# Value columns of an input projection as three split products: the order of work around them and a weight split moved to the next stage

## What is computed

```python
z, xbc, dt_raw, q, k, v, g_out, gk_low = jnp.split(h @ p['w_in'], offsets, axis=-1)
xbc = jax.nn.silu(conv_fn(xbc, p['conv_w'], p['conv_b']))
...
gf = jax.nn.log_sigmoid((gk_low @ p['gk_up_f'] + p['gk_bias_f']).astype(f32)) / GLA_GATE_NORM
...
'v': heads(v, GLA_HEADS, GLA_VAL_DIM),
```

## Time and profile before

| what | value |
|---|---|
| median of 3 runs | 2380.34 us (2379.8 to 2381.73) |
| profiled execution | 2379.42 us, its span 2377.7 us |
| mean granted TensorE clock | 0.949 of 2.4 GHz |
| TensorE (PE) busy | 2166.9 us, 91% |
| VectorE (DVE) busy | 1637.9 us, 69% |
| ScalarE (ACT) busy | 1137.4 us, 48% |
| GpSimd (POOL) busy | 512.4 us, 22% |
| projection, first feature product to first chunk work | 54.1 to 604.1 us of the span |

### The profile page before, as it was taken

How to read it: one execution, slowest core, us unless ns; L and a number is a source line. 1 busy time by engine, 2 the same in 40 slices (tenths; PEclk the granted TensorE clock), 3 DMA queues, 4 the chain that set the end, 5 groups by cost and what they waited for, 6 DMA issues and landing times. The chain is left out here.

```text
span 2377.7 us, 36401 instructions
## 1 busy us (share of the span) xinstructions
PE 2166.9 (91%) x11761; PEld 1711.5 (72%) x11761; DVE 1637.9 (69%) x2101; ACT 1137.4 (48%) x1477; POOL 512.4 (22%) x535
## 2 busy tenths in 40 slices
PE   4999999999899997999997389999999999999980
PEld 2776777777677776888886277787877878878760
DVE  1333333333677667777772889999999999999983
ACT  0222222222555552333332067777777777777763
POOL 1000000000001003233231023333332334334332
PEclk7999999999999996999998699999999999999995
DMA  8223334331598869998873637469978779899957
GB/s 323 67 67 118 117 113 140 119 127 56 182 332 304 293 211 316 315 309 288 301 254 73 233 88 235 129 215 291 327 237 273 222 242 374 273 318 316 373 170 296
DMA packets 208013, 537.25 MB, mean 226 GB/s; under 512 B 14768, under 2 KB 45483, under 8 KB 201387
## 3 DMA queue, kind: packets, MB, share of 16 engines
q1 hardware_dynamic: 174904, 424.71, 49.9%
q0 software_dynamic: 30512, 102.77, 16.5%
q10 hardware_dynamic: 2499, 8.45, 0.9%
HBM read 402.28 MB, written 133.61 MB: 225 GB/s over the span
## 5 line engine op out<-in xcount | busy, mean ns | idle before, releaser
L2180 ACT ACTIVATE w_hi_e<-w_gates 128x2048 fp32r (+1 forms) x103 | 197.9, 1923 | 212.3 <-issue 103.4
L2306 DVE TENSOR_TENSOR w_lo_e<-w_gates,w_hi_e 128x2048 fp32r<-128x2048 f32 x103 | 236.4, 2296 | 33.9 <-ACT w_hi_e L2180 33.9
L2306 DVE TENSOR_TENSOR w_lo_e<-w_ups,w_hi_e 128x2048 fp32r<-128x2048 f32 x102 | 233.3, 2288 | 35.8 <-ACT w_hi_e L2180 35.8
L2306 DVE TENSOR_TENSOR w_lo_e<-w_downs,w_hi_e 128x2048 fp32r<-128x2048 f32 x100 | 228.4, 2284 | 0.0
L2180 ACT ACTIVATE w_hi_e<-w_ups 128x2048 fp32r (+1 forms) x102 | 195.7, 1919 | 23.7 <-PE pd_e L2253 22.5
L2180 ACT ACTIVATE w_hi_e<-w_downs 128x2048 fp32r x100 | 191.6, 1916 | 0.7
L614 PE MATMUL pf<-raws,w_in_sb 128*128 128x256 f32 x800 | 179.0, 387 | 1.1 <-DVE raws L695 1.1
L2253 PE MATMUL pg_e<-w_hi_e,x_hi_e 128*128 128x512 f32 x408 | 167.1, 409 | 7.4 <-DVE w_lo_e L2306 7.4
L614 PEld LDWEIGHTS pf<-raws,w_in_sb 128*128 128x128 f32 x800 | 155.2, 195 | 23.4 <-DVE raws L695 1.5
L2158 POOL DMA_INDIRECT x_mid<-yb_e,to_e x50 | 127.5, 2551 | 187.2 <-DVE yb_e L2350 185.0
L2253 PE MATMUL pd_e<-w_hi_e,h_hi_e 128*128 128x512 f32 x400 | 162.2, 406 | 0.0
(11 more groups left out here) (429 smaller groups left out, 4711.1 us busy)
## 6 DMA issues: line engine op xcount, KB each, us to landing
w_gates<-in_w_gate_dram SPq DMA_DIRECT2D x32, 2048.0 KB, 12.0
w_ups<-in_w_up_dram SPq DMA_DIRECT2D x32, 2048.0 KB
w_downs<-in_w_down_dram SPq DMA_DIRECT2D x32, 2048.0 KB
w_mod_half<-in_w_mod_dram SPq DMA_DIRECT2D x16, 1024.0 KB, 6.6
abc_m<-a_rows SPq DMA_DIRECT2D x16, 1024.0 KB, 4.8
recs<-tok_rec SPq DMA_DIRECT2D x15, 968.0 KB, 7.8
qk_rec<-qk SPq DMA_DIRECT2D x14, 1024.0 KB, 3.9
qk<-qk_rec SPq DMA_DIRECT2D x14, 1024.0 KB
```

The costliest lines, as they stand in the source:

```text
L2180: act.activation(w_hi[:, s % 3:s % 3 + 1, :], raw(part, half, place), ACT.Copy).then_inc(hi_done, 1)
L2306: dve.tensor_tensor(w_lo[:, s % 3:s % 3 + 1, :], raw(part, half, place), w_hi[:, s % 3:s % 3 + 1, :].bitcast(F32), ALU.subtract).then_inc( ...
```

## The change

It does four things.

- The values become split products. `w_in_sb` ends ahead of the value columns. The value weight comes in four chunks of two row blocks through `w_raw`, at the start of `projection`, and is split into `wv_hi` and `wv_lo` (ScalarE, VectorE) in the context group. Each half of a group's tokens is split into `x_hi` and `x_lo` (one buffer each), and the three products go into the same `pz`.
- The first half's values move on TensorE from behind `psm` to between the feature pairs 3 and 4; the transposes of the next inputs stand ahead of the second half's values.
- On ScalarE the second half's high part, SiLU and the next inputs' squares stand ahead of the eviction of feature pair 4.
- `KA` is 0: all 8 row blocks of the gate weight are split in `chunks`; blocks 0 to 2 are loaded in the last but one group of `projection`.

```diff
-KA = 3
+KA = 0
...
-W_LEN = O_G - O_XBC
+W_LEN = O_V - O_XBC
...
-                sp.dma_start(w_in_sb[:, k, :], A["w_in"][0][k * P:(k + 1) * P, O_XBC:O_G]).then_inc(w_in_loaded, 16)
+                sp.dma_start(w_in_sb[:, k, :], A["w_in"][0][k * P:(k + 1) * P, O_XBC:O_V]).then_inc(w_in_loaded, 16)
...
+            def load_v(c):
+                if c >= 3:
+                    sp.wait_ge(wv_lo_done, c - 2)
+                for n in range(2):
+                    k = 2 * c + n
+                    sp.dma_start(w_raw[c % 3][:, n, :], A["w_in"][0][k * P:(k + 1) * P, O_V:O_G]).then_inc(wv_loaded[c % 3], 16)
+            for c in range(3):
+                load_v(c)
...
             sp.dma_start(slab[:, :, :], w_mod_d[EARLY][0]).then_inc(slab_loaded, 16)
+            load_v(3)
...
-                if it == SPLIT - 1:
+                if it == LAT_GROUPS - 1:
+                    sp.wait_ge(wv_lo_done, PAIRS)
                     for k in range(3):
                         load_w(k)
-                if SPLIT <= it < LAT_GROUPS:
-                    sp.wait_ge(K["w_lo_done"], it - SPLIT + 1)
-                    load_w(it - SPLIT + 3)
...
+            def high(it, buf, s):
+                if s:
+                    act.wait_ge(tok_ps, it * 2 + 1)
+                else:
+                    act.wait_ge(ht_done, it * 4 + 4)
+                    if not it == 0:
+                        act.wait_ge(tok_ps, it * 2)
+                act.activation(x_hi[:, :, :], hT[buf][:, :, s * P:(s + 1) * P], ACT.Copy).then_inc(x_hi_done, 1)
+
             def body(it, use, buf, is_ctx, after):
 
+                high(it, buf, 0)
+                if is_ctx:
+                    for c in range(PAIRS):
+                        act.wait_ge(wv_loaded[c % 3], 32 * (c // 3 + 1))
+                        act.activation(wv_hi[:, 2 * c:2 * c + 2, :], w_raw[c % 3], ACT.Copy).then_inc(wv_hi_done, 1)
                 for n in range(5):
+                    if n == 4:
+                        high(it, buf, 1)
+                        act.wait_ge(conv_done, it + 1)
+                        act.activation(fm[:, 0:6, :], fm[:, 0:6, :], ACT.Silu).then_inc(silu_done, 1)
+                        if after is not None:
+                            head(*after)
                     act.wait_ge(feat_ps, it * 5 + (n + 1))
...
-                act.wait_ge(conv_done, it + 1)
-                act.activation(fm[:, 0:6, :], fm[:, 0:6, :], ACT.Silu).then_inc(silu_done, 1)
-                if after is not None:
-                    head(*after)
...
+            def values(it, s, is_ctx):
+                if s == 0 and not is_ctx:
+                    pe.wait_ge(min_done, it * 4)
+                    pe.wait_ge(abs_done, it * 4)
+                if is_ctx:
+                    pe.wait_ge(wv_lo_done, PAIRS)
+                pe.wait_ge(x_lo_done, it * 2 + s + 1)
+                for k in range(KT):
+                    for j, (a, b) in enumerate(((x_hi, wv_hi), (x_hi, wv_lo), (x_lo, wv_hi))):
+                        mm = pe.matmul(pz[s][:, :], a[:, k, :], b[:, k, :], start=(k == 0 and j == 0), stop=(k == KT - 1 and j == 2))
+                mm.then_inc(tok_ps, 1)
...
                 for n in range(5):
+                    if n == 4:
+                        values(it, 0, is_ctx)
...
-                for s in range(2):
...
-                    for k in range(KT):
-                        mm = pe.matmul(pz[s][:, :], h[:, k, s * P:(s + 1) * P], w[:, k, O_V - O_XBC:O_V - O_XBC + GW],
-                                       start=(k == 0), stop=(k == KT - 1))
-                    mm.then_inc(tok_ps, 1)
-                    if after is not None:
-                        turned(*after, range(2 * s, 2 * s + 2))
+                if after is not None:
+                    turned(*after, range(0, 2))
+                values(it, 1, is_ctx)
+                if after is not None:
+                    turned(*after, range(2, 4))
...
+            def low(it, buf, s):
+                dve.wait_ge(x_hi_done, it * 2 + s + 1)
+                dve.tensor_tensor(x_lo[:, :, :], hT[buf][:, :, s * P:(s + 1) * P], x_hi[:, :, :].bitcast(F32), ALU.subtract).then_inc(x_lo_done, 1)
...
+                low(it, buf, 0)
+                if is_ctx:
+                    for c in range(PAIRS):
+                        dve.wait_ge(wv_hi_done, c + 1)
+                        dve.tensor_tensor(wv_lo[:, 2 * c:2 * c + 2, :], w_raw[c % 3], wv_hi[:, 2 * c:2 * c + 2, :].bitcast(F32),
+                                          ALU.subtract).then_inc(wv_lo_done, 1)
...
+                low(it, buf, 1)
                 dve.wait_ge(small_ps, it + 1)
...
-            for k in range(KA + NW, KT):
+            for k in range(NW, KT):
                 sp.wait_ge(w_lo_done, k - NW + 1)
                 load_w(k)
...
-            weights(range(KA, KA + NW))
+            weights(range(NW))
...
-                    weights(range(KA + NW, KT))
+                    weights(range(NW, KT))
```

More of the change, by code:

```diff
@@ L143, in placed @@
             return [where.enter_context(nc.sbuf_tensor(f"{name}{b}", shape, dt, side=side)) for b in range(n)]
-        F32R = mybir.dt.float32r
         recs = placed(spans, "right", "recs", 1, [P, 3 * T_LEN])[0]
@@ L149, in build @@
              "hT": raws[:, 3 * D:].rearrange("p (k c) -> p k c", k=KT),
-             "w_hi": placed(early, "left", "w_zg_hi", 1, [P, KA, 2, SW], F32R),
-             "w_lo": placed(early, "left", "w_zg_lo", 1, [P, KA, 2, SW], F32R),
              "nega": placed(early, "left", "nega", 1, [P, 2 * SH])[0]}
@@ L410, in projection @@
         a_loaded, a_exp, a_done = (sem(n) for n in ("a_loaded", "a_exp", "a_done"))
-        w_raw, w_hi, w_lo = K["w_raw"], K["w_hi"][0], K["w_lo"][0]
-        SPLIT = LAT_GROUPS - KA
+        F32R = mybir.dt.float32r
+        w_raw = K["w_raw"]
+        wv_hi, wv_lo = sb("wv_hi", [P, KT, GW], F32R), sb("wv_lo", [P, KT, GW], F32R)
+        x_hi, x_lo = sb("x_hi", [P, KT, P], F32R), sb("x_lo", [P, KT, P], F32R)
+        wv_loaded = [sem(f"wv{b}_loaded") for b in range(3)]
+        wv_hi_done, wv_lo_done, x_hi_done, x_lo_done = (sem(n) for n in ("wv_hi_done", "wv_lo_done", "x_hi_done", "x_lo_done"))
+        PAIRS = KT // 2
         def before_in(buf, use):
@@ L543, in body @@
                     act.activation(soft[s][:, :], soft[s][:, :], ACT.Ln, bias=1.0).then_inc(ln_done, 1)
[L544 to L547, removed]
             steps(act, head, body)
@@ L629, in body @@
                 mm.then_inc(small_ps, 1)
-                for s in range(2):
-                    if s == 0 and not is_ctx:
-                        pe.wait_ge(min_done, it * 4)
-                        pe.wait_ge(abs_done, it * 4)
-                    for k in range(KT):
-                        mm = pe.matmul(pz[s][:, :], h[:, k, s * P:(s + 1) * P], w[:, k, O_V - O_XBC:O_V - O_XBC + GW],
-                                       start=(k == 0), stop=(k == KT - 1))
-                    mm.then_inc(tok_ps, 1)
-                    if after is not None:
-                        turned(*after, range(2 * s, 2 * s + 2))
+                if after is not None:
[3 more added lines that the diff above has]
+                    turned(*after, range(2, 4))
                 if after is not None:
@@ L772, in body @@
                     dve.tensor_scalar(K["nega"][:, :], K["nega"][:, :], -1.0, None, ALU.mult).then_inc(a_done, 1)
[L773 to L776, removed]
             steps(dve, head, body)
@@ L808, in ps @@
             return ctx.enter_context(nc.psum_tensor(f"{name}_s", [P, 512], F32))
-        w_his, w_los, w_raw = ([K[n][0], sb(n, [P, KT - KA, 2, SW], F32R)] for n in ("w_hi", "w_lo")), None, K["w_raw"]
-        w_his, w_los = w_his
+        w_his, w_los, w_raw = sb("w_hi", [P, KT, 2, SW], F32R), sb("w_lo", [P, KT, 2, SW], F32R), K["w_raw"]
         nega = K["nega"]
         def half(pair, k):
-            return pair[0][:, k, :, :] if k < KA else pair[1][:, k - KA, :, :]
+            return pair[:, k, :, :]
         rec, qk, zg, fc, st = (K[n] for n in ("rec", "qk", "zg", "fc", "st"))
```

## The result

The changed kernel takes **2362.57 us** (median of 4 runs, 2361.94 to 2365.95) where the kernel before takes 2380.07 in the same comparison: ratio 0.993, 95% interval 0.9917 to 0.9942. Run once more, the same kernel took 2365.14 (5 runs), ratio 0.9936 (0.9922 to 0.9949).

The account below looks back on a forecast made before the run. TensorE, busy 91% of the span, was taken as the bound. Terms -23.2 - 5.0 + 12.9 + 5.7 + 1.7 + 0.9 = -7.0 us gave 2372.4 against the profiled execution, 2373.3 against the median; range 2365 to 2380.

Parts of the forecast that it names:

- Value products: TensorE in nine projection groups: 24 split products take 5.63 us instead of 6.97 or 6.87, -23.2 us in all.
- The wait for the next inputs: Before the next inputs' transposes TensorE idles 2.1 us in eight groups, +16.8; old loss of 0.56 goes, -3.9; together +12.9.
- The start: Before the first group: smaller weight blocks load sooner, so VectorE's copy and TensorE's first product come earlier, -5.0 us.
- rival 2: At the start, value chunks share the DMA engines, so little is gained: +3.8 us, 2377.1; chance 0.12.
- The gate weight: Start of chunks: loads and splits of the last blocks form a chain, first gate product ends later, +5.7 us.
- The clock: TensorE's granted clock: one more fall after the new waits, +1.7 us (0 to +13.2), and half a fall in chunks, +0.9.
- Rival 4: The split products run at 215.7 ns each instead of 234: 7.9 us less, 2365.4; chance 0.04.
- Rival 1: Small costs stay out: no more clock falls than before (-2.6), blocks land early in chunks (-2.0): 2368.7; chance 0.25.
- Rival 3: Slower: in latent groups the transposes wait for ScalarE's chain, 2.6 us longer, and the clock falls in all: 2394.4; chance 0.06.
- five signs of being right: Values 5.6 us, first feature near 49, 2.1 us idle before transposes, clean group 59.1, first gate product 5.7 us later.
- those of being wrong: Inputs waiting for GpSimd, third context feature pair waiting, clock falls mid-group in most groups, or first gate product within 3 us.

Follow-up runs that it names:

- b_keep_short: The kernel before with one throwaway float32 product of 512 and one of 256 columns in TensorE's 1.40 us wait per group: 2374.47 us, ratio 0.9978.
- after_again: The changed kernel run and profiled once more, unchanged: 2365.14 us (5 runs), ratio 0.9936 to the kernel before.
- a_old_order: The changed kernel with its split products in the old order of the kernel before, and two raw weight blocks loaded later: 2368.36 us, ratio 0.9957 to the kernel before.
- b_order: The kernel before with the new order alone, its products left as float32: 2408.86 us, ratio 1.013.
- a_between: The changed kernel with the next inputs' first transposes put into the middle of the second half's values: 2351.69 us, ratio 0.9879 to the kernel before.
- a_fill: The changed kernel with transposes inside the second half's values and eight of the next group's feature products in the 1.40 us wait: 2333.51 us, ratio 0.9805 to kernel before.
- a_keep_clock: The changed kernel with throwaway split products in both waits, eight in the 1.93 us and five in the 1.40 us: 2361.14 us, ratio 0.9926 to the kernel before.

## Why the prediction was right and wrong

- *Value products: right, a little too small.* 24 in 5.57 us, forecast 5.63. At the same order the split products are worth 61.45 - 58.68 = 2.77 us a group, forecast 2.58.
- *The wait for the next inputs: right in mechanism, a little too dear.* Releaser and spare time of `rstd` came as forecast. The wait is 1.93, not 2.1, and the order alone costs 1.34 a group, not 1.54: 10.7 instead of 12.9. So groups of 58.7, forecast 59.1. With the products this makes -13.5 over the nine groups, forecast -10.3: 3.2 us of the miss.
- *The start: right*, 4.7 for 5.0 (its other end, where `rstd` binds, is 46.90 - 41.42 = 5.5, not 5.4); rival 2 (value chunks that share the engines) didn't happen.
- *The gate weight: right in mechanism, too cheap.* 8.1 with its share of the clock, forecast 6.6.
- *The clock: the step that failed.* I bounded the falls by "between 0 and 8 more falls, 0 to +13.2" and took one more, +1.7. I wrote that old ones may go, and yet a lower end of 0 left out that they could go on balance. The kernel before paid 6.6 us for the falls in its seven groups (b_keep_short). In the changed kernel 2 or 3 of these groups had one instead of 4, and most falls came behind the order's new wait instead of the old one, where I had added one on top. In the profiled executions the clock came out at -3.6 instead of +1.7: 5.3 us, the largest part of the miss. 1.8 of them are luck: the first features ran at full clock in the profiled execution, and not in after_again, which is the same kernel.
- *The sum of it.* The profiled executions differ by 13.5 us, forecast 7.0. The clock (5.3) and the groups' own terms (3.2) went further down than forecast; chunks (1.5) and the start (0.3) took some of it back. The forecast for the median was off by 10.7. The other 4.3 are the two profiled executions: the one after stood 3.4 above its median, the one before 0.9 below. What made them so isn't known, as only they have a trace.
- *The rivals.* Rival 4's 2365.4 is the nearest number, but it would have been luck: the products take 232 ns, not 215.7. Rival 1 (2368.7) had "no more clock falls than before"; it too held the falls of before for given. Rival 3 (ScalarE's chain) did not happen in the new order; a_old_order shows the chain as the bound in the old one, where I hadn't expected it. The chain of 2.7 us that it names is what "slower" would have taken; the sign would have turned at 2.0 (seven groups, 1.0 beyond the 1 us to spare).
- *The signs.* All five signs of being right came, the last one larger (8.1 us for 5.7), and none of those of being wrong. On the clock they spoke only of more falls, so they could not show this miss.

What decides in which group the clock falls stays open, and so does why the changed kernel has fewer falls than the kernel before: with the same two waits the clock fell twice in each of six groups of b_order and not at all in its seventh. That filling the waits ends the falls in the seven groups is shown by all six runs that filled the waits their order has; a_between, which covers one of them, still falls in three.

## What to carry to other kernels

Price a wait on TensorE twice: once for itself, once for the clock, and let the second price go below nothing, since what it costs now can also go. When an engine's work gets shorter, ask who is late next at the same place: here SiLU's chain and `quarters` kept the transposes waiting 1.80 and 1.93 us, so the two orders came out alike (58.73 and 58.68 us a group), and only work put into the wait gained (a_between, a_fill). A stall of 1 to 2 us can be filled with work from the next round that has its inputs already.

## What was not expected of the hardware

A wait of 1.4 or 1.9 us is followed by a stretch at a lower clock that costs another 1.5 to 1.9 us in some groups, and by none in others with the same rows; in b_order the two together took 3.38 us from each of six groups, more than the order's own 1.34. Throwaway products in these waits held the granted clock at 1.00 for over 400 us on end. And the clock of the first features differs between executions: 1.00 throughout in the first profile of the changed kernel, 0.59 over the first 6 us in a_keep_clock, whose start is the same.
